# RWKV solution and carry products: each 64x64 stationary block as two of 64x32 in neighbouring column sets

## Chip, cores, metric

One core of a Trainium2 chip runs the whole program. The metric is the device time of one execution in microseconds; the median of three runs of the kernel before is 1419.87 us (1419.31 to 1420.28).

## What is computed

Two transformer-like blocks on a sequence of 256 tokens with 1024 channels: feed-forward, a mixer with sparse attention and a short convolution, attention to a memory, feed-forward; then an RWKV-7 time mix, a feed-forward of 4096, windowed attention and again a feed-forward of 4096. The change touches the recurrence of the RWKV time mix alone:

```python
def wkv7(r, w, k, v, a, b):
    '''S_t = S_{t-1} diag(w_t) + (S_{t-1} a_t) b_t^T + v_t k_t^T ;  y_t = S_t r_t'''
    ...
    def step(S, inp):
        r_t, w_t, k_t, v_t, a_t, b_t = inp
        sa = jnp.einsum('bhvk,bhk->bhv', S, a_t)
        S = S * w_t[:, :, None, :] + sa[..., None] * b_t[:, :, None, :] + v_t[..., None] * k_t[:, :, None, :]
        y = jnp.einsum('bhvk,bhk->bhv', S, r_t)
        return S, y
    ...
```

## The kernel before

Outside the recurrence the kernel is a sequence of large products (helper `product`, L290 to L292). Each float32 product is made of three products of split numbers, with 128x128 stationary blocks and 512 moving columns. Weights are loaded by the SyncE queue (L240), split by ScalarE (L263) and VectorE (L279).

The recurrence is solved in chunks of 128 tokens for four heads at a time. With 16 heads and two chunks that makes 8 units, u = 0 to 7. Units alternate between two streams, s = u % 2, with buffers and PSUM banks of their own. A unit does the following. `pe_columns` (L2624) transposes rows to columns and ScalarE copies them (`act_columns`, L2835). `pe_pairs` (L2641) makes the pair products, which VectorE masks (`dve_masks`, L2913). `pe_a_mat` (L2655) makes a transposed matrix. Then two 64x64 triangular matrices per head are inverted by doubling in five levels, n = 0 to 4. In each level `pe_z` (L2669) makes a product, ScalarE copies it (`act_z`, L2849), and `pe_xy` (L2684 and L2688) makes two more. VectorE writes those back under masks (`dve_x`, L2937, and `dve_y`, L2944). `pe_rhs` (L2699, L2702) makes the right hand side, which ScalarE copies (L2853).

The solution of a chunk is made in two halves of 64 tokens. `pe_u_first` (L2712) multiplies the inverse of the first half by its right hand side, and ScalarE copies the result (`act_u`, L2858). `pe_carry` (L2720) makes what the first half gives to the second, and VectorE adds it (`dve_carry`, L2952). `pe_u_second` (L2728) solves the second half, and ScalarE copies it (L2858 again). `pe_y` (L2738 to L2753) makes the output, and for the first chunk the state.

The order on each engine is written out by hand. In `pe_core` the passes u = 1 to 7 interleave the end of unit u - 1 with the start of unit u. In the second half of a pass TensorE does z(u, 1), u_first(u - 1), xy(u, 1), carry(u - 1), z(u, 2), columns(u + 1), u_second(u - 1), xy(u, 2), y(u - 1). After the last pass the three products of unit 7 stand between parts of the output projection (`pe_out_part`, 128x128 blocks). VectorE does the group norm of the first chunk (L3098 to L3143) inside the passes u = 5 to 7. PSUM and operands of the three touched products are plain float32.

In each of the three products the stationary operand is 64 partitions by 64 columns and the moving one 64 partitions by 64 columns, for each of four heads. All four of a call use the same half of the array's rows and the same half of its columns.

Of the kernel before, what the change touches and what calls it, by code (L numbers as in the profile page):

```python
# [26 lines left out]
P = 128  # L27
# [6 lines left out]
HD = 64  # L34
# [38 lines left out]
N_CONST = _at  # L73
LEVELS = 5
HALF = P // 2


def shape_constants():
# [3 lines left out]
    def put(name, a):  # L82
        at, w = CONSTS[name]
        c[:, at:at + w] = a.reshape(P, w)
# [3 lines left out]
    put("ident", eye)  # L88
    put("crossed", np.roll(eye, HALF, 1))
    inv = np.float32(10000.0) ** (-np.arange(0, HD, 2, dtype=np.float32) / np.float32(HD))  # L90
# [14 lines left out]
    strict, full = (s < t).astype(np.float32), (s <= t).astype(np.float32)  # L105
    turned = np.roll(strict, HALF, 1)
    put("upper", np.stack([turned, full, turned, full], 1).astype(np.float32))
    put("pair", (s // HALF == t // HALF).astype(np.float32))
    r, q = (i % HALF)[:, None], np.arange(HALF)[None, :]
    put("ident64", (r == q).astype(np.float32))  # L110
    lev = np.zeros((P, 2, LEVELS + 1, HALF), np.float32)
    for n in range(LEVELS + 1):
# [63 lines left out]
def build(nc, a, out):  # L176
    with ExitStack() as ctx:
        def sb(name, shape, dt=F32):
            return ctx.enter_context(nc.sbuf_tensor("sb_" + name, shape, dt))

        def ps(name, shape):
            return ctx.enter_context(nc.psum_tensor(name, shape, F32))
# [19 lines left out]
        consts = sb("consts", [P, N_CONST])  # L202
        levels = sb("levels", [P, 2, LEVELS + 1, HALF], U8)
        gains = sb("gains", [P, GAIN_ROWS])
# [4 lines left out]
        acc = ps("acc", [P, NT, D])  # L209
# [1856 lines left out]
        class TimeMix:  # L2066
# [639 lines left out]
            def pe_u_first(self, T, u):  # L2706

                s, i, t, g = self.place(u)
                T.e.wait_ge(self.inv_y_done[s], LEVELS * (i + 1))
                T.e.wait_ge(self.rhs_done, u + 1)  # L2710
                for m in range(4):
                    mm = T.e.matmul(acc[0:HALF, s, m * HD:(m + 1) * HD], self.y_inv[s][HALF:P, m, :], self.rhs_buf[s][HALF:P, m, :], start=True, stop=True)  # L2712
                mm.then_inc(*T.one(self.u))

            def pe_carry(self, T, u):

                s = u % 2
                T.e.wait_ge(self.u_done, 2 * u + 1)
                for m in range(4):
                    mm = T.e.matmul(acc[0:HALF, s, 512 + m * HD:512 + (m + 1) * HD], self.mt[s][0:HALF, m, 0, 0:HALF], self.u_buf[s][0:HALF, m, :], start=True, stop=True)  # L2720
                mm.then_inc(*T.one(self.carry))

            def pe_u_second(self, T, u):

                s = u % 2
                T.e.wait_ge(self.carry_done, u + 1)
                for m in range(4):
                    mm = T.e.matmul(acc[HALF:P, s, m * HD:(m + 1) * HD], self.y_inv[s][0:HALF, m, :], self.rhs_buf[s][0:HALF, m, :], start=True, stop=True)  # L2728
                mm.then_inc(*T.one(self.u))

            def pe_y(self, T, u):
# [1067 lines left out]
```

## Time and profile before

| | |
|---|---|
| median of three runs | 1419.87 us (1419.31 to 1420.28) |
| the profiled execution | 1423.15 us |
| its span, first to last instruction | 1421.2 us |
| busy: TensorE, weight load, VectorE, ScalarE | 96%, 79%, 60%, 49% |
| mean granted clock of TensorE | 0.993 |

A matmul's row has a start and a duration; matmuls are pipelined, so the next one starts long before the duration is over. A group "x8" with 0.64 us runs from the first start to the last end. The weight loads (PEld) are rows of their own. A float32 product is recorded as two loads and two matmuls.

### The profile page before, as it was taken

The numbers are of one execution on the slowest core, as the hardware profiler recorded it, in microseconds if no ns is written. First come the engines' busy times: TensorE is split into PE (matmuls) and PEld (weight loads), VectorE is DVE, ScalarE is ACT, GpSimd is POOL, SyncE is SP. The second block draws the span as 40 slices with busy tenths as digits, with TensorE's granted clock in tenths as the row PEclk, the third lists the DMA queues.
The fourth block names the chain that finished last, engine by engine and source line by source line (L and its number), as shares of the span: only waits on it lengthen the run. The fifth ranks groups of instructions, "written<-read, shape, count | busy, mean of one in ns | idle before, by whom it ended". The sixth has DMA issues, their size and how long they took to land.

```text
span 1421.2 us, 23263 instructions
## 1 busy us (share of the span) xinstructions
PE 1368.7 (96%) x8675; PEld 1122.4 (79%) x8675; DVE 857.1 (60%) x1236; ACT 695.7 (49%) x1105; POOL 38.1 (3%) x41
## 2 busy tenths in 40 slices
PE   7999999999999999999899999899999998999998
PEld 5888877878788778888687688668888887788887
DVE  4545568875655465445774788656555576565554
ACT  5444456565465464444554454235444466454442
POOL 0000000000000000000001000110000020000000
PEclk9999999999999999999999999999999999999999
DMA  8655546455444555555352101315555741255552
GB/s 291 215 177 177 182 135 207 153 181 190 160 165 153 159 177 191 198 199 178 122 183 82 54 3 33 110 45 168 187 187 183 238 150 42 78 193 192 179 190 104
DMA packets 145533, 220.51 MB, mean 155 GB/s; under 512 B 16760, under 2 KB 65166, under 8 KB 145328
## 3 DMA queue, kind: packets, MB, share of 16 engines
q1 hardware_dynamic: 145456, 219.43, 47.0%
q8 instruction: 54, 0.88, 0.3%
q14 instruction: 23, 0.19, 0.0%
HBM read 218.33 MB, written 1.05 MB: 154 GB/s over the span
## 4 chain that ended last, share of the span: by engine, by line
PE 87%; DVE 6%; ACT 4%; issue 1%; DMA 1%; SPq 1%; POOL 1%; ACTq 0%; DVEq 0%
PE gp L290 12%; PE acc L290 12%; PE gp L292 12%; PE gp L291 12%; PE acc L292 12%; PE acc L291 12%; PE gp L2669 1%; PE tp L907 1%; PE acc L2684 1%; DMA sb_raw<-in_ffn_w 1%; ACT sb_w_hi L263 1%; DVE sb_w_lo L279 1%; ACT sb_xa_hi L454 1%; PE acc L1226 1%; PE tp L290 1%
## 5 line engine op out<-in xcount | busy, mean ns | idle before, releaser
L279 DVE TENSOR_TENSOR sb_w_lo<-sb_raw,sb_w_hi 128x1024 fp32r<-128x1024 f32 (+1 forms) x380 | 452.4, 1216 | 225.4 <-ACT sb_w_hi L263 223.7
L263 ACT ACTIVATE sb_w_hi<-sb_raw 128x1024 fp32r<-128x1024 f32 (+1 forms) x380 | 388.2, 1053 | 221.0 <-PE acc L292 107.0
L290 PE MATMUL gp<-sb_w_hi,sb_xa_hi 128*128 128x512 f32 (+1 forms) x752 | 301.1, 400 | 13.4 <-DVE sb_xa_lo L461 9.7
L292 PE MATMUL gp<-sb_w_lo,sb_xa_hi 128*128 128x512 f32 (+1 forms) x752 | 293.9, 391 | 0.0
L291 PE MATMUL gp<-sb_w_hi,sb_xa_lo 128*128 128x512 f32 (+1 forms) x752 | 293.3, 390 | 0.0
L290 PEld LDWEIGHTS gp<-sb_w_hi,sb_xa_hi 128*128 128x128 f32 x752 | 142.6, 190 | 47.4 <-issue 10.4
L292 PEld LDWEIGHTS gp<-sb_w_lo,sb_xa_hi 128*128 128x128 f32 x752 | 142.4, 189 | 30.2
L291 PEld LDWEIGHTS gp<-sb_w_hi,sb_xa_lo 128*128 128x128 f32 x752 | 142.7, 190 | 27.4 <-issue 0.5
L290 PE MATMUL acc<-sb_w_hi,sb_mid_hi 128*128 128x512 f32 x408 | 159.1, 390 | 0.0
L292 PE MATMUL acc<-sb_w_lo,sb_mid_hi 128*128 128x512 f32 x408 | 158.9, 389 | 0.0
L291 PE MATMUL acc<-sb_w_hi,sb_mid_lo 128*128 128x512 f32 x408 | 158.7, 389 | 0.0
L784 DVE SCALAR_TENSOR_TENSOR sb_arena<-gp,sb_stat,sb_arena 128x256 f32<-128x256 f32 x44 | 19.6, 481 | 132.9 <-ACT sb_arena L761 132.9
L290 PE MATMUL acc<-sb_w_hi,sb_xa_hi 128*128 128x512 f32 (+1 forms) x240 | 95.3, 397 | 1.5 <-DVE sb_xa_lo L486 1.5
L761 ACT ACTIVATE sb_arena<-gp,sb_stat 128x256 f32<-128x256 f32 x44 | 18.9, 470 | 151.1 <-PE gp L292 151.1
L292 PE MATMUL acc<-sb_w_lo,sb_xa_hi 128*128 128x512 f32 (+1 forms) x240 | 92.1, 384 | 0.0
L291 PE MATMUL acc<-sb_w_hi,sb_xa_lo 128*128 128x512 f32 (+1 forms) x240 | 92.1, 384 | 0.0
L292 PEld LDWEIGHTS acc<-sb_w_lo,sb_mid_hi 128*128 128x128 f32 x408 | 76.6, 188 | 16.0
L291 PEld LDWEIGHTS acc<-sb_w_hi,sb_mid_lo 128*128 128x128 f32 x408 | 76.6, 188 | 15.8
L290 PEld LDWEIGHTS acc<-sb_w_hi,sb_mid_hi 128*128 128x128 f32 x408 | 76.6, 188 | 15.8
L290 PEld LDWEIGHTS acc<-sb_w_hi,sb_xa_hi 128*128 128x128 f32 x240 | 45.4, 189 | 12.3 <-issue 3.4
L292 PEld LDWEIGHTS acc<-sb_w_lo,sb_xa_hi 128*128 128x128 f32 x240 | 45.4, 189 | 9.2
L291 PEld LDWEIGHTS acc<-sb_w_hi,sb_xa_lo 128*128 128x128 f32 x240 | 45.5, 190 | 7.9
(409 smaller groups left out, 1749.6 us busy)
## 6 DMA issues: line engine op xcount, KB each, us to landing
sb_raw<-in_ffn_w SPq DMA_DIRECT2D x264, 256.0 KB, 4.3
sb_raw<-in_mlp_w SPq DMA_DIRECT2D x256, 256.0 KB, 2.9
sb_raw<-in_w_in SPq DMA_DIRECT2D x72, 256.0 KB, 3.1
sb_raw<-in_a_w_rkv SPq DMA_DIRECT2D x48, 256.0 KB, 4.3
sb_raw<-in_xattn_w_kv SPq DMA_DIRECT2D x32, 256.0 KB, 3.3
sb_raw<-in_w_out SPq DMA_DIRECT2D x16, 256.0 KB, 2.9
sb_raw<-in_xattn_w_q SPq DMA_DIRECT2D x16, 256.0 KB, 3.0
sb_raw<-in_xattn_w_o SPq DMA_DIRECT2D x16, 256.0 KB, 2.9
```

What stands on the lines that cost most here:

```text
L263: A.e.activation(w_hi[:, s, :, 0:n], raw[:, r, :, 0:n], ACT.Copy).then_inc(hi_done, 1)
L279: V.e.tensor_tensor(w_lo[:, s, :, 0:n], raw[:, r, :, 0:n], w_hi[:, s, :, 0:n].bitcast(F32), ALU.subtract).then_inc(lo_done, 1)
L290: e.matmul(dst, xh, wh, start=start, stop=False)
L291: e.matmul(dst, xl, wh, start=False, stop=False)
L292: return e.matmul(dst, xh, wl, start=False, stop=stop)
L454: A.e.activation(x[0][:, k, t * P:(t + 1) * P], tp[:, k // 4, (k % 4) * P:(k % 4 + 1) * P], ACT.Copy, scale=gains[:, gain + k:gain + k + 1 ...
L761: A.e.activation(self.silu[:, t, 0:256], gp[:, t, 0:256], ACT.Silu, scale=self.norm.st[:, t:t + 1]).then_inc(self.acted, 1)
L784: V.e.scalar_tensor_tensor(self.mid_rows[:, t, 0:256], gp[:, t, 256:512], self.norm.st[:, t:t + 1], self.silu[:, t, 0:256], ALU.mult, ALU. ...
L907: mm = T.e.transpose(tp[:, b, (2 * j + t) * P:(2 * j + t + 1) * P], self.mid_rows[:, t, at:at + P], ident)
L1226: mm = T.e.matmul(self.side(n)[:, j * self.KEYS[t]:(j + 1) * self.KEYS[t]], q, kk, start=True, stop=True)
L2669: mm = T.e.matmul(gp[there, s, m * HALF:(m + 1) * HALF], self.mt[s][at, m, 0, there], self.x_inv[s][at, m, :], start=True, stop=True)
L2684: mm = T.e.matmul(acc[at, s, 512:1024][:, at_m], self.y_inv[s][there, m, :], self.z_buf[s][there, m, :], start=True, stop=True)
```

## The change

In the three functions each product of a 64x64 stationary block becomes two products of 64x32 blocks: columns 0 to 31 and 32 to 63 of the block, written to neighbouring sets of 32 PSUM partitions. The moving operand is the same for both. Waits and semaphores stay; the increment stays on the last product.

```diff
+QUARTER = P // 4
...
                 for m in range(4):
-                    mm = T.e.matmul(acc[0:HALF, s, m * HD:(m + 1) * HD], self.y_inv[s][HALF:P, m, :], self.rhs_buf[s][HALF:P, m, :], start=True, stop=True)
+                    for q in (0, QUARTER):
+                        mm = T.e.matmul(acc[q:q + QUARTER, s, m * HD:(m + 1) * HD], self.y_inv[s][HALF:P, m, q:q + QUARTER], self.rhs_buf[s][HALF:P, m, :],
+                                        start=True, stop=True)
                 mm.then_inc(*T.one(self.u))
...
                 for m in range(4):
-                    mm = T.e.matmul(acc[0:HALF, s, 512 + m * HD:512 + (m + 1) * HD], self.mt[s][0:HALF, m, 0, 0:HALF], self.u_buf[s][0:HALF, m, :], start=True, stop=True)
+                    for q in (0, QUARTER):
+                        mm = T.e.matmul(acc[q:q + QUARTER, s, 512 + m * HD:512 + (m + 1) * HD], self.mt[s][0:HALF, m, 0, q:q + QUARTER],
+                                        self.u_buf[s][0:HALF, m, :], start=True, stop=True)
                 mm.then_inc(*T.one(self.carry))
...
                 for m in range(4):
-                    mm = T.e.matmul(acc[HALF:P, s, m * HD:(m + 1) * HD], self.y_inv[s][0:HALF, m, :], self.rhs_buf[s][0:HALF, m, :], start=True, stop=True)
+                    for q in (0, QUARTER):
+                        mm = T.e.matmul(acc[HALF + q:HALF + q + QUARTER, s, m * HD:(m + 1) * HD], self.y_inv[s][0:HALF, m, q:q + QUARTER],
+                                        self.rhs_buf[s][0:HALF, m, :], start=True, stop=True)
                 mm.then_inc(*T.one(self.u))
```

## Rows read from the trace of the kernel before

**Rows 1.** The page: shares of the chain that ended last, by engine.
```profile
PE 87%; DVE 6%; ACT 4%; issue 1%; DMA 1%; SPq 1%; POOL 1%; ACTq 0%; DVEq 0%
```

**Rows 2.** Line L2712: records, ns least/median/most, first and last start.
```profile
L2712 PE MATMUL acc<-sb_gain_b,sb_arena x32: 218/218/239, 817.1 to 905.4; 64*64 64x64 f32 x32
```

**Rows 3.** Window of the unit loop: length, each engine's busy us, PEclk, DMA share, GB/s.
```profile
794.00:923.00 129.00, 119.24 (x2758) 99.97 (x2756) 95.06 (x183) 49.04 (x111) 3.80 (x1) 0.99 0.12 40
```

**Rows 4.** Timeline of pass u = 6: start, us, engine, line, [idle before <-releaser].
```profile
889.12 0.68 PE L2669 MATMUL gp<-sb_arena 64*64 64x64 f32 x16
...
889.61 0.54 PEld L2712 LDWEIGHTS acc<-sb_arena,sb_shadow 64*64 64x64 f32 x8
889.64 0.64 PE L2712 MATMUL acc<-sb_arena,sb_shadow 64*64 64x64 f32 x8
889.85 0.38 ACT L2849 ACTIVATE sb_gain_b<-gp 128x256 f32<-128x256 f32 x1 [1.62 <-PE gp L2669]
...
890.34 0.17 PEld L2684 LDWEIGHTS acc<-sb_gain_b,sb_arena 64*64 64x64 f32 x2 [0.20 <-issue]
...
890.84 0.23 PE L2688 MATMUL acc<-sb_arena,sb_gain_b 64*64 64x64 f32 x2
...
891.59 0.54 PEld L2669 LDWEIGHTS gp<-sb_arena 64*64 64x64 f32 x16 [0.19 <-DVE sb_arena L2937]
...
892.69 0.60 PE L2624 MATMUL tp<-sb_consts,sb_arena 128*128 128x128 f32 x4
...
893.22 0.42 PEld L2728 LDWEIGHTS acc<-sb_arena,sb_shadow 64*64 64x64 f32 x6 [0.17 <-issue]
893.39 0.59 ACT L2835 ACTIVATE sb_shade<-tp 128x512 f32<-128x512 f32 x1
...
893.51 0.19 PEld L2684 LDWEIGHTS acc<-sb_gain_b,sb_arena 64*64 64x64 f32 x2
...
893.68 0.22 PE L2728 MATMUL acc<-sb_arena,sb_shadow 64*64 64x64 f32 x1
...
894.43 0.20 PEld L2747 LDWEIGHTS tp<-sb_gain_b,sb_arena 128*64 128x64 f32 x4 [0.21 <-ACT sb_arena L2858]
```

**Rows 5.** Timeline: trains of 128-wide and 32-wide blocks; blocks with one moving column.
```profile
740.14 3.44 PEld L2381 LDWEIGHTS tp<-sb_arena 128*128 128x128 f32 x16
743.91 3.16 PEld L2381 LDWEIGHTS tp<-sb_arena 128*32 128x32 f32 x16 [0.33 <-issue]
...
770.84 1.50 PE L2413 MATMUL tp<-sb_consts,sb_arena 128*128 128x1 f32 x13
```

**Rows 6.** Timeline: calls over several parts of the array.
```profile
884.74 0.46 PE L2655 MATMUL acc<-sb_shade 64*64 64x64 f32 x16 [0.73 <-DVE sb_arena L2913]
...
885.86 0.40 PE L2702 MATMUL tp<-sb_arena,sb_shade 128*64 128x64 f32 x8
```

**Rows 7.** Timeline: the last 128-wide matmuls of L2381 before its 32-wide block.
```profile
743.39 0.59 PE L2381 MATMUL tp<-sb_arena 128*128 128x256 f32 x2
```

**Rows 8.** Chain of pass u = 6 in order of time: start, us, what.
```profile
891.07 0.48 PE acc L2720 x8
...
891.57 0.41 DVE sb_arena L2952
```

**Rows 9.** Timeline: weight load of L2712 in the last unit.
```profile
925.13 0.54 PEld L2712 LDWEIGHTS acc<-sb_arena,sb_shadow 64*64 64x64 f32 x8 [0.36 <-issue]
```

**Rows 10.** Pass u = 7: timeline; windows (PEclk third from last); DMA queues in 901 to 909.
```profile
907.33 0.21 PE L2688 MATMUL acc<-sb_shadow 64*64 64x64 f32 x1 [1.31 <-issue]
...
907.33:913.03 5.70, 5.67 (x130) 5.35 (x130) 4.88 (x8) 0.76 (x2) 0.00 (x0) 0.70 0.33 121
...
909.00:911.00 2.00, 2.00 (x48) 1.88 (x46) 1.97 (x3) 0.76 (x2) 0.00 (x0) 0.50 0.13 45
...
q1 hardware_dynamic: 1538, 2.80, 94.4%
q8 instruction: 1, 0.02, 0.8%
```

## Prediction

> **What bounds the kernel now.** The page first: TensorE is busy 96% of the span, and 87% of the chain that ended last lies on it [rows 1]. The three lines of the change are too small for the page's list, so I asked for them one by one [rows 2]: a product is recorded as two weight loads and two matmuls, and L2712 has 32 matmuls in each of the two streams, 4 units x 4 heads x 2; L2720 and L2728 have as many. A window over the unit loop [rows 3] gives 129 us at clock 0.99. Then one pass in order of time [rows 4]; the other passes repeat it, except where told. The loop is a relay: TensorE finishes a product, ScalarE or VectorE copies it, TensorE goes on. The three lines are fillers in these waits.
>
> **What a call costs now.** L2712 has 8 matmuls in 0.64 us, the last of 0.22 [rows 2, 4]: (0.64 - 0.22)/7 = 0.060 us apart, all in one 64x64 part of the array. Steady trains of other lines tell what sets that [rows 5]. With 256 moving columns, loads of 128-wide blocks are (3.44 - 0.19)/15 = 0.217 us apart (0.19 is one load). The 32-wide train of 16, whose first two loads went in at once, takes 3.16, so 14 steps of about 0.217. The width of the block doesn't enter, the moving columns do. With one moving column and 128-wide blocks the step is (1.50 - 0.25)/12 = 0.104 us (0.25 is one matmul), which is the load alone. For 64 columns the load side is 0.104/2 = 0.052 and the moving side 0.217/4 = 0.054: equal. A 32-wide block halves the load but streams all 64 moving columns again. So a half keeps a step of 0.054 or more: **a call can't get shorter than 8 steps, it can only run two such trains side by side**.
>
> Do they? L2655 uses all four 64x64 parts: (0.46 - 0.22)/15 = 0.016 us apart, a quarter of 0.06. L2702 has 128-row blocks in two column sets, so that its neighbours share every row: (0.40 - 0.22)/7 = 0.026, half of 0.06 [rows 6]. Column sets that share rows do overlap. No row shows two 32-wide sets within 64 columns. From below, a call would be 8 x 0.026 = 0.2 us shorter if the load alone set the step; from above, 8 steps of 0.058 = 0.46 us longer if the halves took turns. I take zero, by L2702, the nearest row.
>
> **What is added: shape changes.** Where the block's shape changes, the next load waits. From 128x128 to 128x32, columns alone differing: the last wide matmul ends at 743.39 + 0.59 = 743.98, the first narrow load starts at 743.91, 0.33 us idle before it [rows 5, 7]. From 128x128 to 64x64: end 892.69 + 0.60 = 893.29, load 893.22 [rows 4]. Both 0.07 us before the end; within one shape L2712's load starts at 889.61, 0.19 before L2669's end at 889.12 + 0.68 = 889.80. So **64x64 to 64x32 costs a drain, and so does the way back**. The first load after it isn't covered, but is 0.026 us shorter for 32 columns. The Trainium skill, "TensorEngine Tiling (Array Packing)", Key Properties, says that changing the tiling mode, not merely the tile, drains TensorE; the trace agrees.
>
> One call after a drain takes, from first load to last matmul's start, 893.68 - 893.22 = 0.46 us, less the shorter load 0.44. With it the five new drains of a pass [rows 4]:
> - u_first. z ends 889.80, load at 889.73, last matmul ends 889.73 + 0.44 + 0.22 = 890.39, next load 890.32 at the earliest. Today L2684's load is at 890.34, behind ScalarE's copy (889.85 + 0.38 = 890.23). **Covered, 0.02 to spare.** ScalarE's copy of the result comes 0.1 later, but its reader, the carry, stands behind L2684 anyway.
> - carry. L2688 ends 891.07, load 891.00, last end 891.66, next load 891.59: today it is at 891.59, behind VectorE's L2937. **Just covered.** But VectorE's own L2952 starts at 891.69 instead of 891.57 [rows 8].
> - u_second. It stands behind columns, where a drain is already. It ends at 893.22 + 0.44 + 0.22 = 893.88, in time for ScalarE (busy to 893.98). But L2684 starts today at 893.51 among its matmuls, in other parts of the array. With another shape it waits to 893.81, needs 0.51 us to its last start (890.34 to 890.85 in the same pass) and ends at 894.54; L2747's load comes at 894.47, today 894.43: **+0.03**.
>
> For the six passes with columns that is 6 x 0.03 = 0.2 us. In passes u = 5 and 6 the chain runs from L2720 through VectorE's L2952 to the group norm and the next masks [rows 8]; there the carry's 0.12 us is on the path: 0.24. Pass u = 7 has no columns and runs at half clock (below): +0.15, from between 0 and 0.3. The last unit's three calls lie between 128x128 products, with drains on both sides already (0.36 us idle before the load, [rows 9]): 3 x 0.02 = 0.07 less. **Sum: 0.2 + 0.24 + 0.15 - 0.07 = +0.5 us.** The cover is the copies of ScalarE and VectorE behind z and x; with none of it, 5 drains x 7 passes x 0.11 us (0.09 to the next step's start, 0.02 of load) = 4 us.
>
> **Against the times.** The profiled execution took 1423.15 us, 1421.2 of it span; it is 3.3 us above the median of the runs shown. The sum gives 1423.65 for it and 1420.4 for the median.
>
> **A side effect: instructions.** 12 more products in a unit, of two loads and two matmuls each, are 8 x 48 = 384 more instructions to read. Once in the loop TensorE stops amid L2688 for 1.31 us on "issue", while weights fill the DMA engines to 94% and one packet of the instruction queue comes in [rows 10]. The granted clock, 0.99 over the loop, is 0.50 (1.2 GHz) from 909 to 911, after that pause. Price: 1.3 us, and at clock 0.70 over 5.70 us at most 0.30 x 5.70 = 1.7 us, so up to 3.0. The borders of the packets move against the code: this stall may go, stay, or come elsewhere.
>
> **The rivals.**
> - *The halves take turns* (the slower side). Each call has 16 steps, 0.46 us more. The slack is 0.02 us at u_first and none at the carry, so it decides from the first step: (7 x 3 + 3) x 0.46 = 11 us, 1431. L2702 and L2655 speak against it. The Trainium skill, "TensorE: Matmul & The Clock Gate", Part 3, says that a weight load overlaps running matmuls only if its row group differs, and the halves share theirs. Here L2702's blocks share all rows and are 0.026 us apart, so the trace speaks against the rule.
> - *Drains uncovered*, where the estimated slack of 0 to 0.02 us is not there: up to 4 us, 1423.9.
> - *The instruction stall goes*: 1420.4 - 3.0 = 1417.4, if nothing else stands in its place and if unprofiled runs have it at all (the 3.3 us between the profiled run and the median leave that open). *A second one comes*: 1423.4.
> - *It works as hoped*, calls 0.2 us shorter. u_first and u_second then still stand beside ScalarE's copies; only the carry's way through VectorE gains, by 2 x 0.2 against the sum, and the 0.03s: 1419.8. Even then nothing can be measured.
>
> **Chances.** Drains mostly covered (the hoped-for case is in it): 0.66. Stall gone 0.13, second stall 0.06, drains uncovered 0.05, turns 0.10. A measurement of this kernel tells 0.2%, 2.84 us, from no change. Faster by more (under 1417.0) only if with the stall something beside it goes: 0.05. Slower (over 1422.7): turns 0.10, and 0.03 each of uncovered drains and second stall: 0.16. The same: 0.79. The range runs from the stall gone, 0.2 to spare, to the second stall, 1417.2 to 1423.4, and leaves out the turns.
>
> **What would show it.** L2712 with 16 matmuls at 64x32 in 0.64 to 0.68 us: the overlap is right; over 1.0 us: turns. Its first load 0.07 us before the end of L2669, and that of L2684 0.07 before its own end: drains. L2684 no longer among L2728. L2952 0.12 us later. The 1.31 us of "issue" gone or elsewhere, and half clock with it. The prediction is wrong if the halves take turns, or if a drain is paid where I count it covered.

## The result and the profile after

| | before | changed |
|---|---|---|
| median, five runs each, side by side | 1420.28 us (1419.31 to 1422.22) | 1426.39 us (1425.39 to 1428.7) |
| ratio, 95% interval | | 1.0037 [1.0026, 1.0048] |
| the same, second series (12 runs of the changed kernel) | 1421.3 us | 1424.29 us, 1.0023 [1.0012, 1.0033] |
| third series (12 runs) | 1421.75 us | 1425.06 us, 1.0026 [1.0017, 1.0036] |
| profiled execution, its span | 1423.15 us, 1421.2 us | 1425.39 us, 1423.4 us |

The change makes the kernel slower by 0.2 to 0.4%, 3 to 6 us. The forecast was 1420.4 us, no change that can be measured, with a range that ended at 1423.4 us. A few executions in the series took far longer (1547.7 to 7705.95 us, of the kernel before, e4 and e15), and the ratios leave them out.

The page of the changed kernel, first: its first line, then the DMA queues (packets, MB, share), then the shares of the chain by engine.

```profile
span 1423.4 us, 23647 instructions
...
q1 hardware_dynamic: 145456, 219.43, 47.4%
q8 instruction: 55, 0.90, 0.3%
...
PE 87%; DVE 7%; ACT 3%; issue 1%; DMA 1%; POOL 1%; SPq 1%; ACTq 0%; DVEq 0%
```

Against [rows 1] the chain has moved by a point from ScalarE to VectorE, no more. The page doesn't find the loss. The first touched line (L2714 now; the three are L2714, L2724 and L2734) by its groups: records, ns least/median/most, first and last start.

```profile
L2714 PEld LDWEIGHTS acc<-sb_gain_b,sb_arena x64: 103/107/108, 814.2 to 904.3; 64*32 64x32 f32 x64
L2714 PE MATMUL acc<-sb_gain_b,sb_arena x64: 215/216/240, 814.2 to 904.4; 64*32 64x64 f32 x64
```

Twice the records of [rows 2], each as long as before: a half costs TensorE a whole matmul. Then pass u = 6 in order of time, the stretch of [rows 4].

```profile
886.39 0.68 PE L2670 MATMUL gp<-sb_arena 64*64 64x64 f32 x16
...
887.00 0.48 PEld L2714 LDWEIGHTS acc<-sb_arena,sb_shadow 64*32 64x32 f32 x16
887.00 0.64 PE L2714 MATMUL acc<-sb_arena,sb_shadow 64*32 64x64 f32 x16
...
887.61 0.17 PEld L2685 LDWEIGHTS acc<-sb_gain_b,sb_arena 64*64 64x64 f32 x2
...
888.27 0.64 PE L2724 MATMUL acc<-sb_arena,sb_shade 64*32 64x64 f32 x16
888.86 0.54 PEld L2670 LDWEIGHTS gp<-sb_arena 64*64 64x64 f32 x16
...
888.95 0.41 DVE L2959 TENSOR_TENSOR sb_arena<-sb_arena,acc 64x256 f32<-64x256 f32 x1
...
890.49 0.48 PEld L2734 LDWEIGHTS acc<-sb_arena,sb_shadow 64*32 64x32 f32 x16 [0.17 <-issue]
...
891.06 0.14 PEld L2685 LDWEIGHTS acc<-sb_gain_b,sb_arena 64*64 64x64 f32 x2
...
891.70 0.20 PEld L2754 LDWEIGHTS tp<-sb_gain_b,sb_arena 128*64 128x64 f32 x4
```

16 matmuls take the 0.64 us that 8 took: (0.64 - 0.22)/15 = 0.028 us apart, half of 0.060. The halves run side by side. Where nothing else holds it, a call that follows a block of another shape loads 0.05 to 0.07 us before the end of what runs: L2714 at 887.00, L2670 ending at 887.07; L2670 at 888.86, with L2724 over at 888.91; L2685 at 891.06, with L2734 over at 891.13. L2685 stands among the matmuls of L2734 no more. From u_second's first load to y's it takes 891.70 - 890.49 = 1.21 us, and 894.43 - 893.22 = 1.21 in [rows 4]. VectorE's add of the carry (L2959) starts 2.56 us behind z, where it was 891.57 - 889.12 = 2.45.

Last, pass u = 7: TensorE's pause, then windows of 2 us (third column from the end: granted clock; then DMA share and GB/s), then the instruction queue from 901 to 907. They answer to [rows 10].

```profile
903.79 0.21 PE L2670 MATMUL gp<-sb_shadow,sb_shade 64*64 64x64 f32 x1 [1.30 <-issue]
...
902.00:904.00 2.00, 0.70 (x18) 0.42 (x17) 0.58 (x2) 0.00 (x0) 0.00 (x0) 1.00 1.03 374
904.00:906.00 2.00, 2.00 (x59) 1.75 (x60) 0.44 (x1) 0.76 (x2) 0.00 (x0) 0.70 1.01 376
906.00:908.00 2.00, 2.00 (x37) 1.71 (x34) 1.38 (x3) 0.37 (x1) 0.00 (x0) 0.50 0.07 27
908.00:910.00 2.00, 2.00 (x48) 1.71 (x46) 2.00 (x3) 0.39 (x2) 0.00 (x0) 0.50 0.04 8
910.00:912.00 2.00, 2.00 (x40) 1.97 (x36) 1.67 (x3) 0.00 (x0) 0.00 (x0) 0.59 0.02 4
...
q8 instruction: 2, 0.03, 2.5%
```

The pause has left xy (L2688) of level 1 and stands in z (L2670) of the same level, some 32 instructions earlier, still amid the weights that fill the DMA engines. TensorE then runs at 0.50, the 1.2 GHz level, till 911.6: 6.8 us, where the trace of before has 3.4.

**A trap in the comparison.** Set side by side, the two first traces put +1.8 us into the unit loop and +3.3 us into the windowed attention near 1200 us, with some of it given back elsewhere. In the second and third trace of the changed kernel, most of the 3.3 us is gone. Stretches of half clock near 205, 250, 498, 690 and 1185 us come and go between executions of one kernel. And the trace of before is of an execution (1423.15 us) 3.3 us above the median of the first three runs. So below I use series of 12 executions (11 of e6), and of the traces only what repeats. The windows show two levels of the granted clock, 1.00 and 0.50, so each execution's mean gives its time at half clock: 2 x (1 - clock) x span. A series' mean of it has a standard error of 0.4 to 2 us.

### The profile page after: what moved, and what is told of

It is laid out like the page before. It is cut to its first block, busy times and chain, and to the rows that moved or that the text cites. A ratio compares the mean times of both kernels' runs of the same rounds, so it can differ in the third digit from the quotient of the medians.

```text
span 1423.4 us, 23647 instructions
## 1 busy us (share of the span) xinstructions
PE 1370.3 (96%) x8867; PEld 1121.2 (79%) x8867; DVE 856.4 (60%) x1236; ACT 695.9 (49%) x1105; POOL 38.1 (3%) x41
## 4 chain that ended last, share of the span: by engine, by line
PE 87%; DVE 7%; ACT 3%; issue 1%; DMA 1%; POOL 1%; SPq 1%; ACTq 0%; DVEq 0%
PE acc L291 12%; PE gp L291 12%; PE acc L293 12%; PE acc L292 12%; PE gp L293 11%; PE gp L292 11%; PE gp L2670 1%; PE tp L908 1%; PE acc L2685 1%; DMA sb_raw<-in_ffn_w 1%; DVE sb_w_lo L280 1%; ACT sb_w_hi L264 1%; ACT sb_xa_hi L455 1%; DVE sb_xa_lo L462 1%; PE acc L1227 1%
## 5 line engine op out<-in xcount | busy, mean ns | idle before, releaser
L291 PE MATMUL acc<-sb_w_hi,sb_xb_hi 128*128 128x512 f32 x120 | 49.5, 412 | 3.4 <-DVE sb_xb_lo L3596 3.4
```

The costliest lines, as they stand in the source:

```text
L291: e.matmul(dst, xh, wh, start=start, stop=False)
```

## The experiments

Two theories stood first. Either the packets of instructions cost it (P: 384 more instructions move all later borders, and the loss at 1200 us follows from their number), or the products themselves do (D: the changes of shape and the doubled matmuls). The runs e1 to e4 went by these. For e5 to e8 the expectations speak of a theory C: the pause in pass u = 7, an instruction packet stuck behind the weights, and the half clock behind it make the loss. The results moved the question to where exactly in pass u = 7 the borders fall. All kernels with a filler do their added products beside the reference's and leave the results unread.

**e1 and e2: instructions alone.** 32 tiny products (128 instructions) behind the right hand side of the last unit, in the kernel before and in the changed one.

```diff
                 self.pe_rhs(T, last)
+                self.pe_filler(T, 32)
```
```python
def pe_filler(self, T, n):
    for k in range(n):
        r, c = (k % 2) * HALF, (k % 2) * HALF + (k // 2 % 2) * (P // 4)
        T.e.matmul(acc[c:c + P // 4, 0, 1020:1021], ident[r:r + HALF, c:c + P // 4], ident[r:r + HALF, r:r + 1], start=True, stop=True)
```

> The kernel before, with 32 tiny float32 products (one moving column, nobody reads them; 128 instructions) in TensorE's 1.6 us wait between the last unit's right hand side and the output projection. 384 instructions of the change are one and a half packets of 256 loads and matmuls (the trace of before has 250 to 260 TensorE records from one instruction packet to the next), so after the loop this kernel's code lies against the packets as the changed kernel's does. Theory P (the packets' borders): the 3.3 us that the changed kernel's trace loses in the windowed attention (1181 to 1226 us) are lost here too: +3 to +3.5 us, near 1423.5. Theory D (drains and calls in the loop cost all of it): no change, within 0.5 us of the kernel before.

Measured: 1421.73 us beside 1421.26, ratio 1.0004 [0.9993, 1.0014]. 384 instructions stand 128 past a multiple of 256, so e1 has, behind the loop, the borders of the changed kernel. Nothing is lost, so moving the borders after the recurrence costs nothing that can be told. The 3.3 us at 1200 us don't come back in the two later traces of the changed kernel either: they were chance.

> The changed kernel with the same 32 tiny products in the same place: 512 instructions more than before, two whole packets, so behind the loop the code lies against the packets as in the kernel before. Theory P: the windowed attention is back to its time of before, 3.3 us less than the changed kernel, near 1422.5 to 1423, +2 us on the kernel before. Theory D: the same as the changed kernel, 1426.4, +6 us.

Measured: 1423.5 us, 1.002 [1.0008, 1.0033]. The loss stays when the later borders are put back where they were. The trace has the changed kernel's pause in z, but no half clock behind it:

```profile
905.57 0.21 PE L2670 MATMUL gp<-sb_shadow,sb_shade 64*64 64x64 f32 x1 [1.49 <-issue]
...
906.00:908.00 2.00, 2.00 (x76) 1.69 (x72) 0.79 (x3) 0.58 (x2) 0.00 (x0) 1.00 0.79 291
```

**e3: the same number of products without a change of shape.** Each 64x64 product is made a second time into the other column half, unread.

```diff
                 for m in range(4):
+                    T.e.matmul(acc[HALF:P, s, m * HD:(m + 1) * HD], self.y_inv[s][HALF:P, m, :], self.rhs_buf[s][HALF:P, m, :], start=True, stop=True)
                     mm = T.e.matmul(acc[0:HALF, s, m * HD:(m + 1) * HD], self.y_inv[s][HALF:P, m, :], self.rhs_buf[s][HALF:P, m, :], start=True, stop=True)
```

> The kernel before with each product of the three calls made twice at 64x64, the second time into the other column half, where nobody reads it: as many instructions as the changed kernel (384 more), no change of shape, no narrow block. Theory P: the same loss in the windowed attention (3.3 us) and the loop's own displaced pause, so +4.5 to +6 us, near the changed kernel. Theory D: the drains are gone, so within 1 us of the kernel before.

Measured: 1423.87 us, 1.0015 [1.0005, 1.0026]. Each pair starts together (start, us):

```profile
860.76 0.22 PE L2712 MATMUL acc<-sb_arena,sb_shadow 64*64 64x64 f32 x1
860.76 0.22 PE L2713 MATMUL acc<-sb_arena,sb_shadow 64*64 64x64 f32 x1
860.82 0.22 PE L2712 MATMUL acc<-sb_arena,sb_shadow 64*64 64x64 f32 x1
```

The doubled products cost next to no time in the loop (from y to y in pass u = 6 it takes 14.58 us, 14.57 before), yet 2 us are lost. There are no drains here. What e3 shares with the changed kernel is the number of instructions up to pass u = 7.

**e4: a split of head 3 alone.** A quarter of the added instructions, but a change of shape within each call too.

```diff
-                    mm = T.e.matmul(acc[0:HALF, s, m * HD:(m + 1) * HD], ...
+                    for q, n in (((0, QUARTER), (QUARTER, QUARTER)) if m == 3 else ((0, HALF),)):
+                        mm = T.e.matmul(acc[q:q + n, s, m * HD:(m + 1) * HD], self.y_inv[s][HALF:P, m, q:q + n], ...
```

> The changed kernel with only the last head's block in two 64x32 halves and the other three at 64x64: the same changes of shape as the changed kernel (even one more within each call), a quarter of the added instructions (96). Theory D: drains cost what they cost in the changed kernel and more, +6 us or over. Theory P: drains cost 0.5 to 2 us (one more per call, partly under copies), and the windowed attention's loss depends on where 96 instructions put the borders, between 0 and 3.3 us; the trace's passes u = 1 to 4 show the drains alone, 14.39 us a pass as before or up to 0.3 us more.

Measured: 1427.11 us, 1.0035 [1.0024, 1.0045].

```profile
859.60 0.76 PE L2714 MATMUL acc<-sb_arena,sb_shadow 64*64 64x64 f32 x10
...
860.87 0.75 PE L2724 MATMUL acc<-sb_arena,sb_shade 64*64 64x64 f32 x10
...
906.03 0.27 PE L2689 MATMUL acc<-sb_arena,sb_gain_b 64*64 64x64 f32 x2 [2.00 <-issue]
```

Ten matmuls take 0.76 us where sixteen took 0.64: the drain within the call costs 0.1. The passes before the group norm joins in take 14.53 us instead of 14.38 to 14.42, so the cover behind the copies is used up with this. A quarter of the instructions and a loss as large: neither theory has it alone, but the pause is the longest of all, 2.00 us, and 10.2 us of half clock follow it.

**e5, e16: the changed kernel again.** Both series are in the table above. They lose 3.0 and 3.3 us. By the bound that the expectation of e5 had set (under 4 us), the first measurement, 6.1 us over five executions, was high.

> The changed kernel once more, beside the next three on one chip. Theory C (pause and clock): +4 to +6 us on the kernel before; its mean granted clock is 0.990 to 0.991 where the kernel before has 0.993, the half clock standing behind TensorE's pause in pass u = 7. The four kernels of the first job spread by 1 to 2 us between runs of one kernel, so less than 4 us would say that the first measurement was high.

> The changed kernel a third time, in one series with its late-weights form: +3 to +4 us over the kernel before, 2 us over the changed kernel with late weights, mean granted clock 0.991.

**e6, e7: no weight burst in pass u = 7.** The weights of the next feed-forward, which SyncE asks for at about 900 us, wait for the outputs of the recurrence.

```diff
             tmix.sp(sp)
+            sp.wait_ge(tmix.y_done, 2 * tmix.GROUPS - 1)
             mlp1.sp(sp)
```

> The kernel before; SyncE waits for the output of unit 6 before it issues the first loads of the next feed-forward's weights, so that the burst of weights (901 to 909 us in the trace of before) comes after the pause's place. Theory C: an instruction packet stuck behind the burst makes the pause; without it the 1.31 us of issue and the half clock of 909 to 912 go, 1 to 3 us faster than the kernel before (1.3 for the pause, up to 1.7 for the clock). Rival theory (the pause is the packet's own cost, whatever the burst): pause and time stay, within 0.5 us, or the late weights cost time at 945 us.

Measured: 1420.3 us beside 1421.3, 0.9988 [0.998, 0.9997], faster than both kernels.

> The changed kernel with the same late weights. Theory C: the pause is gone, so that only drains remain: 0.5 to 1.5 us over e6_before_late, and 4 to 5 us under the changed kernel. Rival theory (drains and narrow blocks cost it in every pass): as far above e6_before_late as the changed kernel is above the kernel before, 5 us.

Measured: 1421.55 us, 0.9997 [0.9987, 1.0008]. With one line the changed kernel loses nothing against before; against e6 it stands 1.25 us higher. The expected "pause is gone" didn't come: two small ones stay. The changed products in pass u = 7, z of level 2 to y, of e6 and then of e7:

```profile
905.30 0.68 PE L2669 MATMUL gp<-sb_shadow,sb_shade 64*64 64x64 f32 x16
905.82 0.64 PE L2728 MATMUL acc<-sb_gain_b,sb_arena 64*64 64x64 f32 x8
906.56 0.27 PE L2684 MATMUL acc<-sb_shadow 64*64 64x64 f32 x2
...
907.19 0.44 PE L2747 MATMUL tp<-sb_gain_b,sb_shade 128*64 128x128 f32 x4
```
```profile
906.25 0.68 PE L2670 MATMUL gp<-sb_shadow,sb_shade 64*64 64x64 f32 x16
906.86 0.64 PE L2734 MATMUL acc<-sb_gain_b,sb_arena 64*32 64x64 f32 x16
907.50 0.27 PE L2685 MATMUL acc<-sb_shadow 64*64 64x64 f32 x2
...
908.45 0.33 PE L2689 MATMUL acc<-sb_shadow 64*64 64x64 f32 x2 [0.25 <-issue]
908.70 0.44 PE L2754 MATMUL tp<-sb_gain_b,sb_shade 128*64 128x128 f32 x4
```

Up to xy both take the same: 906.56 - 905.30 = 1.26 us, 907.50 - 906.25 = 1.25. u_second comes 0.09 later behind its drain, and xy waited for ScalarE's copy anyway. From there to y it is 1.20 us against 0.63. Most of that is the small pause inside xy: its last two matmuls start 0.95 us behind its first, 0.47 in e6. So a pause puts what follows back by more than the row's idle time, here by 0.48 us for 0.25.

**e8 and e12: where in the loop.** In e8 unit 6 (pass u = 7) keeps its 64x64 products, in e12 it alone has the narrow ones.

```diff
-                    for q in (0, QUARTER):
+                    for q, n in (((0, HALF),) if u == 6 else ((0, QUARTER), (QUARTER, QUARTER))):
```

> The changed kernel with unit 6, whose calls stand in pass u = 7 beside the pause, left at 64x64 blocks; the seven other units are split. Theory C with the narrow blocks holding the clock down behind the pause: 3 to 4 us back, +1 to +2 us on the kernel before, clock 0.993. Rival theory (all passes alike): one eighth of the loss back, +4.5 to +5 us.

Measured: 1422.71 us, 1.001 [1.0002, 1.0019]; the pause is 1.20 us in L2670, with 3.4 us of half clock behind it.

> The kernel before with the three calls of unit 6 alone made as 64x32 pairs, those of pass u = 7; the complement of the kernel that left unit 6 as it was. 48 more instructions, all of them in pass u = 7. Theory that pass u = 7 holds most of the loss, because its drains have no columns to hide behind and because the half clock lasts longer with these calls: +1.5 to +2.5 us. Rival, that the loss is spread over all passes or comes with the number of instructions: +0.2 to +0.6 us. From z(6,2) to y in pass u = 7 both expect 2.3 to 2.5 us instead of 1.9.

Measured: 1423.68 us, 1.0015 [1.0005, 1.0025]. One eighth of the change loses no less than the other seven (e8). The pause of e12 is in u_first itself and is longer:

```profile
905.06 0.24 PE L2714 MATMUL acc<-sb_gain_b,sb_arena 64*32 64x64 f32 x1 [1.68 <-issue]
...
905.00:907.00 2.00, 1.94 (x51) 1.58 (x53) 0.44 (x1) 0.38 (x1) 0.00 (x0) 0.68 0.79 286
907.00:909.00 2.00, 2.00 (x36) 1.71 (x36) 1.92 (x4) 0.38 (x1) 0.00 (x0) 0.50 0.03 10
```

Its 16 added instructions of u_first moved the border there. This fits the products' theory and that of the borders alike, so the next two take the products away.

**e9: the kernel before again.** Ratio 1.0 [0.9987, 1.0013]; its pause is 0.70 us, in L2688 as before, with no half clock behind it. The 1.31 us that I priced were of one execution.

> The kernel before, unchanged, once more: how much two series of one kernel differ, and whether its trace keeps the pause and the half clock of pass u = 7. Expected on either theory: ratio 1.000 within 0.001, an idle stretch of 0.5 to 1.3 us in TensorE's stream between 902 and 907 us, and half clock behind it for 0 to 3.4 us.

**e10 and e11: the borders alone.** The changed kernel's page has 55 packets with 0.90 MB, 16 KB each. The Trainium skill, "Runtime: NRT & Kernel Launch", Instruction fetch mechanics, gives 16 KiB as 256 instructions and says that the cost of crossing such a border is mostly hidden. Ahead of the recurrence e10 puts 12 tiny products (48 instructions, written to a spare column of tp) into the kernel before, and e11 puts 52 (208) into the changed one, where 288 + 208 = 496 are then added up to z of pass u = 7, and 512 behind u_first.

```diff
             def pe_core(self, T):
+                self.pe_filler(T, 12)
                 self.pe_columns(T, 0)
```

> The kernel before with 12 tiny float32 products (48 instructions, about 1 us of TensorE in all, results unread) ahead of the first transposes of the recurrence. Up to the pause of pass u = 7 the change adds 304 instructions, which is 48 more than 256; if instructions are read in packets of a size that divides 256, this kernel has its packet borders where the changed kernel has them, with none of the changed products. Theory that the place of the borders makes the pause longer (the changed kernel's cost in pass u = 7 is the instructions'): idle stretch of 1.3 us or more, half clock of 6 us behind it, and +1 to +2 us in the median. Rival, that the changed products themselves are what costs there: +0 to +0.5 us over the kernel before, half clock as before.

Measured: 1423.75 us beside 1421.69, 1.0016 [1.0006, 1.0025]. Its pause and windows:

```profile
903.89 0.44 PE L2669 MATMUL gp<-sb_shadow,sb_shade 64*64 64x64 f32 x7
905.85 0.34 PE L2669 MATMUL gp<-sb_shadow,sb_shade 64*64 64x64 f32 x5 [1.52 <-issue]
...
906.00:908.00 2.00, 1.89 (x57) 1.78 (x54) 0.40 (x1) 0.76 (x2) 0.00 (x0) 0.91 1.04 399
908.00:910.00 2.00, 2.00 (x35) 2.00 (x38) 1.67 (x4) 0.39 (x1) 0.00 (x0) 0.50 0.30 111
910.00:912.00 2.00, 2.00 (x51) 1.88 (x48) 2.00 (x4) 0.38 (x1) 0.00 (x0) 0.50 0.00 0
912.00:914.00 2.00, 2.00 (x36) 1.88 (x34) 1.40 (x2) 0.28 (x1) 0.00 (x0) 0.50 0.05 12
```

Not one product of the recurrence is changed here, and there is the pause in z, 1.52 us, 6.8 us of half clock behind it, and 2.1 us more time: what the changed kernel's traces show.

> The changed kernel with 52 tiny float32 products (208 instructions, some 2 us of TensorE where the stream may or may not wait, results unread) ahead of the first transposes of the recurrence, so that 512 instructions are added up to the pause of pass u = 7 and the borders stand where the kernel before has them. Theory of the borders: 1 to 2 us less than the changed kernel, 1422.5 to 1424 less the filler's own 0 to 2 us. Rival, changed products: no less than the changed kernel, 1424.5 to 1428.

Measured: 1422.98 us, 1.0007 [0.9996, 1.0017], with granted clock 0.9930 over 12 runs, as before. The pause is back in xy:

```profile
905.25 0.21 PE L2689 MATMUL acc<-sb_shadow 64*64 64x64 f32 x1 [1.07 <-issue]
```

With all changed products in place, most of the loss is gone, though it is told only across series: the interval reaches up to where the last one of the changed kernel, 1.0026 [1.0017, 1.0036], begins. The place fits a period of 256 to the matmul. With 288 instructions added up to there, 15 matmuls of z come before the pause (changed kernel, e2, e3, e8). With 48 added (e10) it is 7, which is 16 instructions earlier, and 48 is 16 more than 288 - 256. With 512 the pause is behind the same matmuls of xy as without any. The trace agrees with the 256 of the Trainium skill's page; "mostly hidden" doesn't hold amid this burst.

**e13 to e15: both together.** Late weights with and without e10's 48 instructions, and the changed kernel with late weights.

> The kernel before with the next feed-forward's weights loaded late (as in the run named before_late) and with the 12 tiny products (48 instructions, results unread) ahead of the recurrence, which alone cost 2.1 us. Theory that the instructions' place costs only where instruction reading meets the weight burst: nothing is left of it, the same as late weights without the filler, 1420 to 1421, granted clock 0.993 or more, no pause in pass u = 7. Rival, that it acts elsewhere (in the products at 690 us or the windowed attention at 1184 us): 2 us more than late weights alone, 1422 to 1423, clock 0.991.

> The kernel before with late weights once more: 1 to 1.5 us under the kernel before if its gain is real (0.9988 in the first series), within 0.5 us of it if that was chance.

> The changed kernel with late weights once more: the drains' own cost is its distance from the run before it. From the traces (0.10 us in pass u = 6, 0.57 in pass u = 7, little elsewhere) 0.7 us; from the first series 1.0 to 1.3 us.

Measured beside 1421.75: e13 1420.14 us, 0.9993 [0.9984, 1.0002]; e14 1420.46 us, 0.9994 [0.9986, 1.0003]; e15 1421.57 us, 1.0005 [0.9994, 1.0015]. The 48 instructions that cost 2.1 us under the burst cost nothing without it. The changed kernel with its burst (e16) stands 3.5 us above e15, where I expected 2. e13's pause, and the windows behind it:

```profile
903.05 0.45 PE L2669 MATMUL gp<-sb_shadow,sb_shade 64*64 64x64 f32 x9 [0.71 <-issue]
...
902.00:904.00 2.00, 1.26 (x24) 0.99 (x24) 0.66 (x2) 0.38 (x1) 0.00 (x0) 1.00 0.00 0
904.00:906.00 2.00, 1.87 (x60) 1.76 (x61) 1.16 (x3) 0.38 (x1) 0.00 (x0) 1.00 0.04 8
906.00:908.00 2.00, 1.88 (x61) 1.71 (x61) 1.97 (x3) 0.76 (x2) 0.00 (x0) 1.00 0.00 0
```

Here my expectation of no pause was wrong: one of 0.71 us stays with no weights under way, and the clock stays at 2.4 GHz.

All together, by where the pause of pass u = 7 lies (level 1 unless told; idle us of the one trace; half clock per execution is the mean of a series):

| kernel | pause lies in | idle | ratio | half clock |
|---|---|---|---|---|
| before (e9) | xy | 1.31 (0.70) | 1 | 20 us |
| e1 | xy | 0.48 | 1.0004 | 20 us |
| e11, changed | xy | 1.07 | 1.0007 | 20 us |
| changed (e5, e16) | z | 1.30 (1.57, 1.19) | 1.0037 (1.0023, 1.0026) | 27 us (25, 26) |
| e2, changed | z; xy of level 2 | 1.49; 0.51 | 1.002 | 24 us |
| e3, doubled | z | 1.36 | 1.0015 | 21 us |
| e8, changed but unit 6 | z | 1.20 | 1.001 | 23 us |
| e10, before + 48 | z | 1.52 | 1.0016 | 27 us |
| e12, unit 6 only | u_first | 1.68 | 1.0015 | 25 us |
| e4, head 3 only | the end of level 0's xy, just ahead of z | 2.00 | 1.0035 | 27 us |
| e6, e14, late | none | - | 0.9988, 0.9994 | 19, 18 us |
| e13, late, before + 48 | z | 0.71 | 0.9993 | 19 us |
| e7, e15, late, changed | z; xy of level 2 | 0.20, 0.12; 0.25, 0.80 | 0.9997, 1.0005 | 16, 20 us |

Under the burst, every kernel whose pause left the xy of level 1 lost 1 us or more, and none of those where it stayed can be told from no change.

## Why the prediction was wrong

**What a call costs: right.** Halves side by side, 0.64 us for 16, in the value I took (0.64 to 0.68). The rival of the turns (1431 us) is out, and so, for these blocks, is the Trainium skill's rule ("TensorE: Matmul & The Clock Gate", Part 3) that a load overlaps running matmuls only if its row group differs: the halves share all rows and start 0.028 us apart.

**Drains: right in kind, too high in size.** All stand where they were foretold, 0.05 to 0.07 us before an end. u_first and carry are covered. The 0.03 at u_second (0.04 by its own terms, 894.47 - 894.43), six times, came to 0.00 in pass u = 6 (1.21 us both times). The carry's way through VectorE was put at 2 x 0.12 us. It shows where the next masks come late: TensorE's idle time ahead of a_mat in passes u = 6 and 7, of e6, then of e7.

```profile
883.00 0.46 PE L2655 MATMUL acc<-sb_shade 64*64 64x64 f32 x16 [0.73 <-DVE sb_arena L2913]
898.32 0.46 PE L2655 MATMUL acc<-sb_shade 64*64 64x64 f32 x16 [1.49 <-DVE sb_shade L2913]
```
```profile
883.57 0.46 PE L2656 MATMUL acc<-sb_shade 64*64 64x64 f32 x16 [0.84 <-DVE sb_arena L2920]
898.99 0.46 PE L2656 MATMUL acc<-sb_shade 64*64 64x64 f32 x16 [1.59 <-DVE sb_shade L2920]
```

0.11 and 0.10 us: the mechanism, the place and the size. The last unit's saving of 0.07 came to 0.10: from u_first to y it takes 928.79 - 922.32 = 6.47 us in e7 and 927.56 - 920.99 = 6.57 in e6. Pass u = 7 was put at +0.15. From z of level 1 to y it is 0.83 us longer in e7 than in e6 (5.32 and 4.49) and 1.31 longer in e15 than in e14 (5.78 and 4.47). The two small pauses there put what follows back by 0.42 + 0.48 and 0.32 + 1.02 us, so hardly anything is left for drains. Their sum in the traces is thus near 0.1 us where I had 0.5.

In the series the late-weight pairs differ by 1.25 and 1.1 us (e7 to e6, e15 to e14), and 0.8 to 1.3 us of pauses account for nearly all of it. In e6 the matmul at the border of before starts only 0.10 us late. The pauses stand where the count of added instructions puts the borders (z of level 1, and some 256 instructions on, the end of level 2's xy). That is read off four traces and not shown by a run, since e13 has such a pause, too, and lost nothing.

**The instructions: this step failed.** The pause was found, its tie to the weights' burst too, and that the borders would move ("go, stay, or come elsewhere"). But the cases were only "goes" (0.13) and "a second one comes" (0.06). That it merely moves was put at nothing, without a reason, and left within the 0.66 of the likeliest case. It isn't free. Three things were sized wrong:
- The base. 1.31 us is a long pause for the kernel before (0.48 and 0.70 in e1 and e9), so there was more room above than the one trace told: in the changed kernel 1.19 to 1.57.
- The half clock behind it. I bounded it by 0.30 x 5.70 = 1.7 us from a trace with 3.4 us of it. It lasts 6.8 us in all three traces of the changed kernel (none in e2's). Over a series an execution of before spends 20 us at half clock and one of the changed kernel 25 to 27.
- The sum of this alone is e10's: +2.1 us, ratio 1.0016. With the late pairs' 1.1 to 1.25 us it gives 3.2 to 3.3 us; the series have 3.0, 3.3 and, in the first and shortest, 6.1. The other 3 us of that first series no run explains; single executions of one kernel differ with a standard deviation of 1.1 to 2.1 us.

**The reference point.** The three runs that I built on (1419.87 us) were low. In four series of 35 executions the kernel before has a median of 1421.26 to 1421.75 us, 1.4 to 1.9 us above it. In the first series, which had 1420.28 us, only 0.4 of the 6.0 us of miss is the reference's. Even from there +0.5 us is wrong by 2.5 to 2.8 us in the later series and 5.6 in the first, so the slower side, held to 0.16, was given too little, not just a size misjudged.

**What stays open.** Why a pause in z costs more than one in xy isn't settled. In e10 and in the changed kernel it is longer and followed by more half clock; but e8, with the same border as the changed kernel, lost less (1.0010), so the narrow products of unit 6 may add to the time at half clock (23 us against 25 to 27, each to within 1 to 2 us: not shown), and e11's single trace has 6.8 us of half clock in this place, too, while its series as a whole has no more than before. e2 has the pause in z, 1.49 us, and no half clock, so its length alone doesn't decide whether the clock falls. In e12 the border is as many instructions behind the start of z as in the kernel before (64 by count), yet in the last matmul of u_first it made a pause of 1.68 us. An estimate from the series of the kernel before: there 1 us more at half clock goes with 0.2 to 0.3 us more time. So e10's 7 us more stand for 1.3 to 2 us of its 2.1, but e3's 1.4 us more for 0.4 at most of its 2; where the rest of e3's loss lies isn't known. Nor does a trace tell how often each length occurs: for this only the means over a series speak.

**The better version** is e6: one wait on SyncE's queue, 0.9988 [0.998, 0.9997] in one series and 0.9994 [0.9986, 1.0003] in another. It takes away the burst and with it most of the pause; the gain of 1.0 to 1.3 us is at the edge of what can be told.

## What to carry over

Splitting a block into column sets doubles the matmuls that stream the same columns, so it won nothing here, where the moving side already set the step; it only adds changes of shape, each a drain of about 0.1 us here that is free just while a copy of another engine covers it. Added instructions are not free either: count them up to each place where TensorE stands on "issue" while a DMA burst runs, and price a pause that moves by its own range over several executions, the half clock behind it included. For a loss of 0.2%, put some unread instructions (48 here) ahead of the old kernel before blaming the new code, and move the burst rather than the code.

## What was not expected of the hardware

- The place of a packet border counts for 2.1 us in 1421: 48 instructions of unread products some 100 us earlier move TensorE's pause from xy to z, 1.52 us long, with a DMA share of 1.01 to 1.04 around it (e10). Without the burst it is 0.71 us and the clock stays up (e13).
- Column sets that share all rows overlap fully: 0.028 us per 64x32 matmul (x16 in 0.64 us), and two 64x64 products side by side start within 0.01 us of each other (e3).
- A change of shape inside a call costs about 0.1 us even from 64x64 to 64x32 in the same half of the array: 10 matmuls in 0.76 us (e4).
- Behind pauses of 1.07 to 2.00 us amid the burst came 3.4 to 10.2 us at half clock, but behind e2's of 1.49 us none, nor behind 0.48 and 0.70 us (e1, e9).
- The same program's time at half clock moves by itself: stretches of 3.4 to 10.2 us came and went between executions, and one trace of before and one of the changed kernel differ by 3.3 us in a stretch that the change doesn't touch.
